# Two late pairs of experts trade their way of adding rows, the row additions come pair by pair in three buffers, and the token counts follow the first pair

## The chip, the core and the metric

The kernel runs on one core of one Trainium2 chip. The time is that of one execution on the device, in microseconds (us). A second clock value used below is the span: the time from the first to the last instruction that the profiler recorded.

## The reference, cut to what matters

Two transformer-like blocks work on a sequence of 512 tokens of width 1024, in f32. The first has attention, a recurrent branch and an MLP; the second has a Fourier and a state space branch and then a mixture of 64 experts. The change touches only the experts:

```
g_prob = softmax(ht @ wg + bg);  p_g, g_idx = top_k(g_prob, 1)          # one of 8 groups
e_logits = (ht @ we + be).reshape(t, 8, 8)                              # 8 experts in each
top_l, top_i = top_k(e_logits of the group, 2)                          # two experts a token
gate_w = p_g * softmax(top_l)
...
def expert_block(xb, e):
    a = silu(xb @ w_gate[e]) * (xb @ w_up[e])                           # 1024 -> 512
    return a @ w_down[e]                                                # 512 -> 1024
out = sum over the token's two experts of gate_w * expert's row
x = x + out;   return rms_norm(x)
```

There are 512 tokens with 2 experts each, so 1024 rows go through experts. Every expert has three matrices of 2 MB.

## The kernel before

**Pairs.** The 64 experts are worked on in 32 pairs, q = 0 to 31. An expert gets up to 64 rows (CAP), so that a pair fills 128 columns of TensorE. For a pair TensorE (in `pe_pair`) turns the gathered rows (`xt`), multiplies by the two gate matrices (`g`, 32 matmuls of 64 columns each, L1201), by the two up matrices (`u`, 32 more of L1201), turns the activated rows (`at`, L1212) and multiplies by the two down matrices (`d`, two halves nh = 0 and 1 of the 1024 columns, L1238; in the last pair L1226). VectorE scales `xt` (L2704, `dve_xt`), makes the gated product (L2709 and L2714), and copies half of the result to YE (`dve_ye`); ScalarE makes the tanh (L1679), copies `aT` (L1683) and the other half of YE (L1690).

**Weights.** SyncE's queue brings the matrices into a ring of ten slots of 2 MB (RING). Matrix n goes into its slot when TensorE has used matrix n - 10. The eleventh and twelfth come in pieces; the eleventh's first half goes to FIRST_HALF, a region that lies over constants which are no longer needed (from the constant `c01` on). That load (L3072) waits for the matmuls that count the tokens of each expert (`cnt`, L1133), since their operand `ones` lies in the region.

**Two ways to add a pair's rows.** For a pair in SPREAD, VectorE makes four one-hot matrices (`dve_hots`, L2647) and TensorE multiplies them with YE: 8 matmuls of 128x512, one for each half of each of four blocks of 128 tokens (`pe_spread`, L1172). VectorE adds each to the residual X (`dve_spread`, L2640). These 8 stand in the next pair's program: 4 ahead of its `g`, 2 between `u` and `at`, 2 between `at` and `d`; those of the last pair stand behind and between its own `d`. For a pair in STORED, GpSimd scatters YE to `y_d` in HBM by an indirect DMA (L2901, semaphore `y_st`). When all ten are written, GpSimd gathers the stored rows again (L2897): 8 indirect DMAs, one for each block of 128 tokens and each of the token's two experts; rows that belong to no stored pair are skipped. VectorE adds each gathered tile to X with its weight (`dve_comb`, L2631, 128x1024). GpSimd's queue also gathers each pair's tokens (L2897 from `hn_d`), except the first pair's, which come from one-hots.

**The end.** Before the change the 8 gathers start when the scatter of pair 30 has landed, into eight buffers YA; VectorE adds all 8 in the last pair (q = 31) ahead of adding the spread of pair 31. Then come the sums of squares, the scale and the stores of the output. The last pair's up matrices land as one load of 2 MB and two of 1 MB (semaphores `up0`, `up1`, `up2`, L3082 and L3085), its down matrices in six pieces (`last0` to `last2`, L3092).

```
STORED = [0, 2, 6, 10, 14, 18, 22, 26, 29, 30]
SPREAD = [q for q in range(PAIRS) if q not in STORED]
```

## Time and profile before

| | |
|---|---|
| time, median of 3 executions | 2291.91 us (2291.58 to 2294.2) |
| the profiled execution's own time | 2294.22 us |
| its span | 2292.3 us |
| TensorE busy, share of the span | 97% |
| VectorE, ScalarE, GpSimd busy | 43%, 15%, 13% |
| mean granted TensorE clock | 0.991 |
| HBM read and written | 558.63 MB and 24.67 MB |

The pairs of experts run from about 1345 us to 2276 us of the span. TensorE's busy share is that of a pipelined engine whose ends are modelled, so it tells only where it stands idle. In that stretch the granted clock and the share of the 16 DMA engines, by slices, say more.

### The profile page before, as it was taken

Reading aid. Unit: us, or ns where it says so; the run is one execution under the profiler, and the core shown is the slowest. Engines: PE = TensorE matmul, PEld = TensorE weight load, DVE = VectorE, ACT = ScalarE, POOL = GpSimd, SP = SyncE. Lnnn points to the kernel's source line nnn. Section 1 sums busy time; section 2 is a strip of 40 time slices with the busy share of each in tenths; the row PEclk is TensorE's granted clock in tenths of the full one; section 3 lists DMA queues with packets and bytes.
Section 4 is the critical chain, followed back from the end, with each engine's and each line's share of the span. In section 5 each row is a group of like instructions: output and inputs, shape, how many; then the busy total and the mean of one; then the engine's idle time right before and its main releaser. Section 6 shows DMA issues by size and latency. Waiting matters only on the chain.

```text
span 2292.3 us, 23432 instructions
## 1 busy us (share of the span) xinstructions
PE 2212.3 (97%) x9146; PEld 1140.7 (50%) x9146; DVE 974.5 (43%) x1888; ACT 349.0 (15%) x677; POOL 291.7 (13%) x254
## 2 busy tenths in 40 slices
PE   9999999999999999999999999999999999989996
PEld 6544444485888544477578553333333333333332
DVE  2246544541875587536544442222222222223124
ACT  2025324301222200021111210000000000000001
POOL 0002112221276100001053010000000000000001
PEclk9999999999999999999999999999999999999998
DMA  7211110230243444482432589999999999999996
GB/s 292 101 56 47 55 46 10 111 137 29 95 138 124 173 188 166 167 154 109 154 138 111 238 321 424 427 427 426 425 427 427 425 427 426 428 427 426 427 426 251
DMA packets 74991, 561.86 MB, mean 245 GB/s; under 512 B 20786, under 2 KB 25522, under 8 KB 42432
## 3 DMA queue, kind: packets, MB, share of 16 engines
q1 hardware_dynamic: 52688, 530.70, 57.8%
q10 hardware_dynamic: 15136, 22.75, 3.0%
q0 software_dynamic: 7056, 6.89, 0.9%
q8 instruction: 75, 1.23, 0.2%
q14 instruction: 36, 0.29, 0.0%
HBM read 558.63 MB, written 24.67 MB: 254 GB/s over the span
## 4 chain that ended last, share of the span: by engine, by line
PE 79%; DMA 13%; DVE 6%; issue 1%; ACT 1%; SPq 0%; POOL 0%; DVEq 0%; ACTq 0%; POOLq 0%
PE ps L1201 13%; DMA sb<-in_eu 11%; PE ps L527 9%; PE ps L855 8%; PE ps L1238 8%; PE ps L434 7%; PE ps L776 5%; PE ps L1172 5%; PE ps L1011 5%; PE ps L459 3%; PE ps L1039 2%; PE ps L737 2%; DVE sb L1717 2%; PE ps L715 2%; DMA sb<-in_ed 2%
## 5 line engine op out<-in xcount | busy, mean ns | idle before, releaser
L1201 PE MATMUL ps<-sb 128*64 128x512 f32 x2048 | 453.9, 599 | 22.6 <-DMA sb<-in_eu 17.4
L1201 PEld LDWEIGHTS ps<-sb 128*64 128x64 f32 x2048 | 156.6, 138 | 310.1 <-issue 310.1
L1717 DVE TENSOR_TENSOR sb<-sb 128x1024 f32<-128x1024 f32 (+9 forms) x420 | 226.9, 573 | 86.3 <-PE ps L855 38.3
L527 PE MATMUL ps<-sb 128*128 128x512 f32 x512 | 237.7, 602 | 0.0
L1238 PE MATMUL ps<-sb 128*64 128x512 f32 x992 | 224.5, 606 | 9.6 <-ACT sb L1683 5.5
L855 PE MATMUL ps<-sb 128*128 128x512 f32 x448 | 193.4, 592 | 1.4 <-DVE sb L2268 1.4
L434 PE MATMUL ps<-sb 128*128 128x512 f32 (+1 forms) x464 | 189.2, 567 | 0.9 <-issue 0.9
L776 PE MATMUL ps<-sb 128*128 128x256 f32 x784 | 175.5, 383 | 3.6 <-DVE sb L2188 3.6
L1172 PE MATMUL ps<-sb 128*128 128x512 f32 x352 | 164.6, 599 | 2.2 <-issue 2.2
L776 PEld LDWEIGHTS ps<-sb 128*128 128x128 f32 x784 | 148.4, 191 | 25.1 <-DVE sb L2188 4.0
L1238 PEld LDWEIGHTS ps<-sb 128*64 128x64 f32 x992 | 70.4, 139 | 154.3 <-issue 145.7
L527 PEld LDWEIGHTS ps<-sb 128*128 128x128 f32 x512 | 91.5, 191 | 101.3 <-issue 99.5
L855 PEld LDWEIGHTS ps<-sb 128*128 128x128 f32 x448 | 84.6, 190 | 106.7 <-issue 106.7
L2640 DVE TENSOR_TENSOR sb<-sb,ps 128x512 f32<-128x512 f32 x176 | 120.6, 688 | 38.8 <-PE ps L1172 38.5
L434 PEld LDWEIGHTS ps<-sb 128*128 128x128 f32 x464 | 87.5, 190 | 96.5 <-issue 92.7
L2709 DVE SCALAR_TENSOR_TENSOR sb<-sb,ps 128x512 f32<-128x512 f32 x32 | 22.1, 690 | 219.5 <-ACT sb L1679 219.4
L1011 PE MATMUL ps<-sb 128*128 128x256 f32 x504 | 109.2, 379 | 0.9 <-issue 0.9
L2714 DVE SCALAR_TENSOR_TENSOR sb<-sb,ps 128x512 f32<-128x512 f32 x32 | 22.1, 690 | 204.8 <-PE ps L1201 204.8
L2897 POOL DMA_INDIRECT sb<-hn_d,sb x31 | 31.1, 1005 | 582.1 <-PE ps L1183 548.0
L1011 PEld LDWEIGHTS ps<-sb 128*128 128x128 f32 x504 | 95.7, 190 | 14.6 <-issue 1.7
L1271 ACT ACTIVATE sb<-ps 128x512 f32<-128x512 f32 (+3 forms) x98 | 51.5, 535 | 321.4 <-PE ps L434 54.3
L1172 PEld LDWEIGHTS ps<-sb 128*128 128x128 f32 x352 | 61.8, 191 | 74.6 <-issue 74.6
(349 smaller groups left out, 2062.4 us busy)
## 6 DMA issues: line engine op xcount, KB each, us to landing
sb<-in_eu SPq DMA_DIRECT2D x63, 2048.0 KB, 33.9
sb<-in_eg SPq DMA_DIRECT2D x62, 2048.0 KB, 35.5
sb<-in_ed SPq DMA_DIRECT2D x60, 2048.0 KB, 33.7
sb<-in_m SPq DMA_DIRECT2D x16, 2048.0 KB, 7.3
sb<-in_m SPq DMA_DIRECT2D x16, 1024.0 KB, 4.9
sb<-in_mg SPq DMA_DIRECT2D x8, 1536.0 KB, 6.6
sb<-in_wo SPq DMA_DIRECT2D x4, 2048.0 KB, 7.9
sb<-in_winF SPq DMA_DIRECT2D x12, 512.0 KB, 3.5
```

What stands on the lines that cost most here:

```text
L434: ins = pe.matmul(out, lhsT, rhs, start=k == 0, stop=k == len(pieces) - 1)
L459: ins = pe.matmul(T.ap(*tile)[:, t], lhsT, rhs[:, t], start=k == 0, stop=k == 7)
L527: ins = pe.matmul(o, lhsT, rhs, start=k == 0, stop=k == 7)
L776: ins = pe.matmul(T.ap(*name)[:, 256 * (f % 2):256 * (f % 2) + 256], a[:, j], b[:, j], start=j == 0, stop=j == 3)
L855: ins = pe.matmul(T.ap("m2", turn, f), a[j], b[j], start=s_ == 0 and j == 0, stop=s_ == 7 and j == 1)
L1011: ins = pe.matmul(o[:, 256 * f:256 * f + 256], a[:, j], b[:, j], start=j == 0, stop=j == n - 1)
L1172: pe.matmul(o, OH[o_ % 2][:, i, :], YE[:, 512 * nh:512 * nh + 512], start=True, stop=True).then_inc(T.f("sp", q, i, nh), 1)
L1201: ins = pe.matmul(o[64 * e:64 * e + 64, :], x[:, k, 64 * e:64 * e + 64], weight(2 * mat + e, 512 * k), start=k == 0, stop=k == 7)
L1238: ins = pe.matmul(o[64 * e:64 * e + 64, :], aT[:, k, 64 * e:64 * e + 64], weight(4 + e, d), start=k == 0, stop=k == 3)
L1271: act.activation(dst, T.ap(*name) if src is None else src, ACT.Copy).then_inc(T.s(*name), 1)
L1717: return own(dve.tensor_tensor(o, a, b, op))
L2640: dve.tensor_tensor(xs, xs, T.ap("sp", q, i, nh), ALU.add).then_inc(S("xadd") if q == PAIRS - 1 else T.s("sp", q, i, nh), 1)
```

## The change

The list of stored pairs ends in 26, 27, 28, and no longer in 26, 29, 30. So pairs 27 and 28 are now scattered to HBM, and 29 and 30 are spread by one-hots; there are ten stored and 22 spread pairs as before. The 8 gathers of stored rows use three buffers in turn, and a gather waits until the addition that used its buffer is done. VectorE makes additions 0 to 2 in pair 29, 3 to 5 in pair 30, 6 and 7 in pair 31. The count matmuls move behind the first pair, and the VectorE operations that make the number of rounds of them (`count_rounds`) with them. The constant `ones` moves ahead of `c01`, out of the region under FIRST_HALF, and that load waits for TensorE's last read of the region (`rows_read`) instead of the counts.

```diff
-STORED = [0, 2, 6, 10, 14, 18, 22, 26, 29, 30]
+STORED = [0, 2, 6, 10, 14, 18, 22, 26, 27, 28]
...
-        YA = [view(done_ck, 0, 1024), view(done_ck, 1024, 1024), view(zone, xt0 + 1024, 1024), XG[0]]
-        YA += [view(EXTRA[0], 1024 * n, 1024) for n in range(4)]
+        YA = [view(done_ck, 0, 1024), view(done_ck, 1024, 1024), view(zone, xt0 + 1024, 1024)]
+        ROWS = {PAIRS - 3: range(3), PAIRS - 2: range(3, 6), PAIRS - 1: range(6, 8)}
...
+                    if i == 2 and k == 7:
+                        ins.then_inc(S("rows_read"), 1)
...
             first_rows(2, 1)
-            open_tile(pe, ("cnt",), 4)
-            for j in range(4):
-                ins = pe.matmul(T.ap("cnt")[:, 0:64], ck("ones"), ES[:, j, :], start=j == 0, stop=j == 3)
-            ins.then_inc(T.f("cnt"), 1)
...
                 if q == 0:
+                    o = open_tile(pe, ("cnt",), any_bank())
+                    for j in range(4):
+                        ins = pe.matmul(o[:, 0:64], ck("ones"), ES[:, j, :], start=j == 0, stop=j == 3)
+                    ins.then_inc(T.f("cnt"), 1)
                     o = open_tile(pe, ("wtab",), any_bank())
...
             def weights():
-                count_rounds()
...
                     copy(("wtab",), WTAB, T.ap("wtab")[:, 0:PAIRS])
+                    count_rounds()
...
             dve_xt(dve, T, q)
+            dve_spread(dve, q - 1, TILES[0:4])
             dve_gate(dve, T, q)
             dve_up(dve, T, q)
+            dve_spread(dve, q - 1, TILES[4:8])
             dve_hots(dve, q)
-            if len(SPREAD) > 1:
-                for i, nh in TILES:
-                    dve.wait_ge(*T.free("sp", SPREAD[-2], i, nh))
-            for n in range(8):
-                dve_comb(dve, n, S("comb"), YA[n], S(f"comb{n}"))
-            dve.wait_ge(S("comb"), 8)
+            dve_stored_rows(dve, q)
...
+                if q >= PAIRS - 3:
+                    dve.wait_ge(S("comb"), 8 if q == PAIRS - 1 else ROWS[q + 1].start)
...
+            if table is T and q in ROWS:
+                dve_stored_rows(dve, q)
             dve_ye(dve, table, q)
+
+        def dve_stored_rows(dve, q):
+            done = [p for p in SPREAD if p < q]
+            for i, nh in TILES:
+                dve.wait_ge(*T.free("sp", done[-1], i, nh))
+            for n in ROWS[q]:
+                dve_comb(dve, n, S("comb"), YA[n % 3], S(f"comb{n}"))
...
             for n in range(8):
-                if n == 4:
-                    pool.wait_ge(*T.full("u", PAIRS - 2))
-                gather(pool, YA[n], y_d, GY[:, n % 2, n // 2:n // 2 + 1], 1023, S(f"comb{n}"))
+                if n > 2:
+                    pool.wait_ge(S("comb"), n - 2)
+                gather(pool, YA[n % 3], y_d, GY[:, n % 2, n // 2:n // 2 + 1], 1023, S(f"comb{n}"))
...
-                    sp.wait_ge(*T.full("cnt"))
+                    sp.wait_ge(S("rows_read"), 1)
```

The first place is the end of TensorE's program. Before the change its rows for pairs 30 and 31 read as follows, where L1183 turns `xt`, L1201 is `g` with `u`, L1212 is `at`, L1238 and L1226 are `d`, and L1172 is a spread:

```order
L1183 MATMUL ps<-sb 128x128 x8
L1201 MATMUL ps<-sb 64x512 x32
L1212 MATMUL ps<-sb 128x128 x4
L1238 MATMUL ps<-sb 64x512 x16
L1183 MATMUL ps<-sb 128x128 x8
L1201 MATMUL ps<-sb 64x512 x32
L1212 MATMUL ps<-sb 128x128 x4
L1226 MATMUL ps<-sb 64x512 x8
L1172 MATMUL ps<-sb 128x512 x2
```

After the change (two lines further down in the file) the last pair's rows are these, and pair 30's begin in the same way:

```order
L1185 MATMUL ps<-sb 128x128 x8
L1174 MATMUL ps<-sb 128x512 x4
L1203 MATMUL ps<-sb 64x512 x32
L1174 MATMUL ps<-sb 128x512 x2
L1214 MATMUL ps<-sb 128x128 x4
L1174 MATMUL ps<-sb 128x512 x2
L1228 MATMUL ps<-sb 64x512 x8
L1174 MATMUL ps<-sb 128x512 x2
```

Eight spread matmuls have come into each of the pairs 30 and 31, and have gone out of pairs 28 and 29 (the rows of pair 29 now read as those of pair 30 before).

The second place is GpSimd's queue over the last pairs, where L2901 (now L2911) is a scatter and L2897 (now L2907) a gather. Before:

```order
L2897 DMA sb<-hn_d,sb 128x1024 x3
L2901 DMA y_d<-sb 1024x1024 x2
L2897 DMA sb<-y_d,sb 128x1024 x8
```

After the change:

```order
L2911 DMA y_d<-sb 1024x1024
L2907 DMA sb<-hn_d,sb 128x1024
L2911 DMA y_d<-sb 1024x1024
L2907 DMA sb<-hn_d,sb 128x1024
L2907 DMA sb<-y_d,sb 128x1024 x8
```

The last two scatters stand ahead of the last gather of a pair's tokens (pair 31's), and the eight gathers of stored rows follow right behind it, in pair 29's time.

The third place is VectorE's end, from the one-hots of the last pair on, where L2631 is an addition of stored rows. Before:

```order
L2647 TENSOR_SCALAR sb<-sb 128x128 x4
L2631 SCALAR_TENSOR_TENSOR sb<-sb 128x1024 x8
L2640 TENSOR_TENSOR sb<-sb,ps 128x512 x4
L2623 TENSOR_SCALAR sb<-ps,sb 128x512
L2640 TENSOR_TENSOR sb<-sb,ps 128x512 x4
```

After the change (L2648, L2630, L2641, L2622):

```order
L2648 TENSOR_SCALAR sb<-sb 128x128 x4
L2630 SCALAR_TENSOR_TENSOR sb<-sb 128x1024 x2
L2641 TENSOR_TENSOR sb<-sb,ps 128x512 x4
L2622 TENSOR_SCALAR sb<-ps,sb 128x512
L2641 TENSOR_TENSOR sb<-sb,ps 128x512 x4
```

Two of the eight additions are left there; three stand in pair 29 and three in pair 30, behind the one-hots of these pairs and ahead of the copy to YE.

## Rows read from the trace of the kernel before

**Rows 1.** The page: span, GB/s in 40 slices, the software queue, a load's landing.
```profile
span 2292.3 us, 23432 instructions
...
GB/s 292 101 56 47 55 46 10 111 137 29 95 138 124 173 188 166 167 154 109 154 138 111 238 321 424 427 427 426 425 427 427 425 427 426 428 427 426 427 426 251
...
q0 software_dynamic: 7056, 6.89, 0.9%
...
sb<-in_m SPq DMA_DIRECT2D x16, 2048.0 KB, 7.3
```
**Rows 2.** Timeline of TensorE in pair 29: start, time, line, operation.
```profile
2185.09 1.09 PE L1183 MATMUL ps<-sb 128*128 128x128 f32 x8
...
2189.55 13.95 PE L1201 MATMUL ps<-sb 128*64 128x512 f32 x64
...
2207.55 7.09 PE L1238 MATMUL ps<-sb 128*64 128x512 f32 x32
2214.56 1.09 PE L1183 MATMUL ps<-sb 128*128 128x128 f32 x8
```
**Rows 3.** The same in pairs 30 and 31; idle time before and its ending in brackets.
```profile
2224.86 7.09 PE L1201 MATMUL ps<-sb 128*64 128x512 f32 x32 [1.61 <-DMA sb<-in_eu]
...
2236.35 8.52 PE L1238 MATMUL ps<-sb 128*64 128x512 f32 x32 [2.73 <-DMA sb<-in_ed]
...
2246.40 7.09 PE L1201 MATMUL ps<-sb 128*64 128x512 f32 x32 [0.51 <-DVE sb L2704]
2254.03 7.09 PE L1201 MATMUL ps<-sb 128*64 128x512 f32 x32 [0.54 <-DMA sb<-in_eu]
...
2263.47 3.65 PE L1226 MATMUL ps<-sb 128*64 128x512 f32 x16 [0.69 <-ACT sb L1683]
...
2276.91 3.67 PE L1172 MATMUL ps<-sb 128*128 128x512 f32 x8 [1.34 <-issue]
```
**Rows 4.** DMA issues at 2215.1 and 2187.0 us: count, KB, us to landing.
```profile
sb<-in_eu SPq DMA_DIRECT2D x1, 1024.0 KB, 38.9
...
sb<-hn_d,sb POOLq DMA_INDIRECT x1, 11.0
```
**Rows 5.** Windows: busy time of each engine, granted clock, DMA share, GB/s.
```profile
1340.00:1350.00 10.00, 10.00 (x67) 6.39 (x68) 8.48 (x38) 0.32 (x2) 1.02 (x2) 1.00 0.98 393
...
2180.00:2235.00 55.00, 50.55 (x225) 19.05 (x220) 12.23 (x18) 3.68 (x6) 2.00 (x2) 1.00 1.01 427
2235.00:2240.00 5.00, 3.65 (x12) 1.31 (x14) 0.00 (x0) 0.00 (x0) 0.00 (x0) 0.66 1.00 426
...
2260.00:2265.00 5.00, 3.37 (x18) 1.36 (x16) 3.66 (x7) 0.60 (x1) 4.05 (x3) 1.00 1.01 374
2265.00:2270.00 5.00, 4.16 (x16) 1.26 (x14) 4.58 (x5) 2.18 (x3) 1.10 (x1) 1.00 0.47 147
```
**Rows 6.** Timeline of VectorE and GpSimd from 2254 us on.
```profile
2254.86 1.03 POOL L2897 DMA_INDIRECT sb<-y_d,sb  x1 [7.50 <-DMA y_d<-sb]
...
2262.62 11.02 DVE L2631 SCALAR_TENSOR_TENSOR sb<-sb 128x1024 f32<-128x1024 f32 x8
...
2276.06 0.75 DVE L2623 TENSOR_SCALAR sb<-ps,sb 128x512 f32<-128x512 f32 x1
```
**Rows 7.** Timeline of all engines ahead of the first pair.
```profile
1340.86 1.00 PE L1133 MATMUL ps<-sb 128*128 128x64 f32 x8
...
1341.83 0.29 DVE L2553 TENSOR_TENSOR sb<-sb 128x128 f32<-128x128 f32 x1
...
1342.26 2.02 PE L1095 MATMUL ps<-sb 128*128 128x128 f32 x16
...
1345.24 0.22 DVE L2575 TENSOR_REDUCE sb<-ps 128x1 f32<-128x64 f32 x1
...
1345.87 0.15 DVE L2579 TENSOR_SCALAR sb<-sb 128x1 int32<-128x1 int32 x1
```
**Rows 8.** DMA issues at 1378.4 us, behind the gate matmuls of pair 1.
```profile
sb<-in_ed SPq DMA_DIRECT2D x2, 2048.0 KB, 11.3
```

More of the change, by code:

```diff
@@ L41 @@
 CK_COLS = {}
-CK_N = _cols(CK_COLS, [("ident", 128), ("iota", 128), ("tok", 8), ("gf", 8), ("gx", 8), ("kept", 32), ("c01", 124), ("tri", 128), ("ones", 128),
+CK_N = _cols(CK_COLS, [("ident", 128), ("iota", 128), ("tok", 8), ("gf", 8), ("gx", 8), ("kept", 32), ("ones", 128), ("c01", 124), ("tri", 128),
                        ("neg", 128), ("cneg", 124), ("cs", 256), ("pad", 40)])
```

## The prediction

> **What bounds the kernel now.** I read the page first, for the traffic in 40 slices; then the timeline of TensorE over the last three pairs, for what it waits for; then the landings of the loads, and the timelines of VectorE and GpSimd at the end. From the 25th slice on the DMA engines move 425 to 428 GB/s in every slice but the last [rows 1], and in the windows their share is 1.01 [rows 5]: they are full. TensorE's waits in pairs 30 and 31 are ended by the weights: 1.61 us ahead of `u` and 2.73 ahead of `d` in pair 30, 0.54 ahead of `u` in pair 31 [rows 3]. A load of the last pair lands 38.9 us after its issue [rows 4], so the queue holds over 30 us of work and TensorE can be late by some us without leaving it empty. So the end of the kernel hangs on when the last pair's first up pieces land, and on what TensorE still has to do from there. VectorE and GpSimd matter only where they hold up this chain.
>
> From `u` of pair 31 at 2254.03 us it runs to `d` at 2263.47 [rows 3], 9.44 us later, and from there 28.8 us to the end of the span at 2292.3. I keep this last part as it is, but for one item below, and ask by how much the start of the last `d` moves.
>
> **The change part by part.**
>
> *Gathers of stored rows, moved ahead of the last weights.* Before, the first of 8 is issued at 2254.86 [rows 6], when the up matrices that `u` needs have landed (2215.1 + 38.9 = 2254.0 [rows 4]). They take bandwidth only from the last down matrices, and no wait of the last `d` is put down to these [rows 3]. After, the last scatter (pair 28) lands two pairs earlier, and gathers 0 to 2 run in pair 29, 3 to 5 behind the first additions, 6 and 7 behind those of pair 30. A gather lands 11.0 us after its issue while the loads take over 30 [rows 4]: it doesn't queue behind them but takes its share at once. All 8 thus come ahead of the last up pieces, 6 of them ahead of pair 30's down matrices. The two scatters that move were ahead of these before too and cost the same.
>
> Their size: GpSimd's queue moves 6.89 MB [rows 1]. The gathers of tokens of pairs 1 to 31 are 31/32 of 1024 rows of 4 KB, 4.06 MB; the other 2.83 MB are scatters and gathers of the same stored rows, 1.41 MB each. At the stream's 427 GB/s that is 3.3 us. At this queue's own use of the engines, 0.9% of 2292.3 us for 6.89 MB or 3.0 us a MB [rows 1], it is 4.2 us. No row isolates them in a full stream, so I take the middle, 3.7. The same queue's mixed window at the end, 374 GB/s at a share of 1.01 [rows 5], says that the upper half is no less likely.
>
> The Trainium skill, "DMA: Bandwidth & Descriptors", section "Anatomy of one DMA", fits the moving part of a DMA by bytes at 436 GB/s, which would make 3.2 us of the 1.41 MB and an end 0.5 us earlier than by my 3.7; the 374 GB/s above, with much small traffic in it, disagree.
>
> *Spreads in pairs 30 and 31.* The lists of instructions show 8 more matmuls in each, and 8 fewer in pairs 28 and 29, which wait for weights anyway or gain time that is lost again at the next landing. The price is read from pair 29, which has them: from the start of L1183 to `g` 4.46 us (2185.09 to 2189.55), from `g` to `d` 18.00 (2189.55 to 2207.55), from `d` to the next L1183 7.01 [rows 2]. From the start of `u` to `d` it is 18.00 less half of L1201's 13.95, 11.03 us, against 9.44 without spreads: 1.6 more.
>
> *The sum, by two chains.* By the weights: `u` of pair 31 at 2254.03 + 3.7 = 2257.7, and `d` 11.03 later, at 2268.8. By TensorE: `d` of pair 30 at 2236.35 + 3.7 x 6/8 = 2239.1, next L1183 + 7.01, `g` + 4.46, `d` + 18.00, together 29.47: 2268.6. Both agree, so neither covers the other. The last `d` comes at 2268.8 instead of 2263.47: **+5.3**. In pair 30 TensorE itself is not what holds `d`: pair 29 without spreads ends earlier than before.
>
> *Eight additions of VectorE.* Before they are one block of 11.02 us up to 2273.64, 1.38 each; behind it come four spreads, and the copy of the second half of YE starts at 2276.06 [rows 6], though its matmuls had ended at 2276.91 - 1.34 = 2275.57 [rows 3]. With two additions left that copy follows at once, about 0.1 us after the matmuls: **-0.4**. In pairs 29 and 30 three additions, 4.1 us, stand ahead of the copy to YE. The spread that reads it comes 7.01 + 1.09 = 8.1 us after `d` starts [rows 2], which leaves 4 us for the one-hots and the copy: nothing, while the gathers have landed.
>
> *The first load of the ring's third round.* It is issued when the counts have ended, some 0.9 us later than it could be (1.00 us of L1133 [rows 7]). But at that time the DMA share is 0.98 [rows 5], and the next pieces wait for TensorE's first pair. That pair doesn't start earlier: the matmuls at 1342.26 need the product of VectorE that ends at 1342.12 [rows 7]. I take 0; the other end is -0.9, the whole stream moved.
>
> *The counts behind pair 0.* TensorE's 1.00 us and VectorE's, from 1345.24 to 1346.02, 0.8 us [rows 7], now both stand ahead of pair 1's `g`: up to 1.8 us. The load that waits for these gate matmuls goes at 1378.4. Two loads into an empty queue would land 7.3 us and 7.3 + 4.9 after their issue (2 MB at 427 GB/s are 4.9), on the median 9.75; they took 11.3 [rows 1, 8], so 1.55 us were queued ahead. So 0.2 us of the stream may be lost: **+0.2**, between 0 and 1.8. The lateness of TensorE itself goes away in its later waits for weights.
>
> Together 5.3 - 0.4 + 0.2 = **+5.1 us**: the profiled execution would go from a span of 2292.3 to 2297.4 and from its own 2294.2 to 2299.3. That execution was the slowest of the three and 2.3 above their median; on the median 2291.91 it makes **2297.0**. With the gathers at 3.3 us the sum is +4.7, at 4.2 it is +5.6.
>
> **The rivals.**
>
> *A, on the other side: the gathers take nothing from the weights* (they use gaps within packets that a share of 1.01 doesn't show). Then TensorE's chain decides: 2236.35 + 29.47 = 2265.8, +2.35, less 0.4, makes 2293.9, which is no change that can be told. For it speaks that the engines' share is a sum of packet times and can count waiting; against it that GB/s doesn't rise when this queue has work [rows 5]. It decides from a cost of the gathers below 3.2 us: under that the total is under 4.6. Chance 0.20.
>
> *B, the clock.* Between 2235 and 2240 the granted clock averages 0.66 [rows 5], after idle stretches of 1.61 and 2.73 us; `d` of pair 30 ran 8.52 us, not 7.09 [rows 3]. The 7.01 above is at full clock. If half clock comes again there, or in pair 31, it is on the path now and costs 1.4: 2298.4. TensorE has less idle time in pair 30 than before, some 2 us ahead of `u`, which speaks against it. Chance 0.17.
>
> *C, additions that wait for their gathers.* If gathers 0 to 2 land too late for pair 29, VectorE holds up the copy to YE, with it the spread of pair 29 and `g` of pair 30. Beyond some 2 us this reaches `u`: 2299. Against it: 11.0 us a gather from the middle of pair 29's time still leaves some. Chance 0.06.
>
> *D, the stream moves with its first load* by the full 0.9 and nothing else changes: 5.1 - 0.2 - 0.9 = +4.0, 2295.9. Against it the share of 0.98. Together with other gains that I don't see, some even beyond, chance 0.07.
>
> **How the numbers follow.** A measurement of this kernel tells about 0.2%, 4.6 us, from no change; the three runs lie 2.6 us apart. The forecast has 0.50; as its sum runs from +4.7 to +5.6, and a run can come out half a us to one us otherwise, I give 0.37 of it to slower and 0.13 to within 0.2%. A is within (0.20), B and C are slower (0.23), of D and unseen gains 0.03 is within and 0.04 faster. So faster 0.04, same 0.36, slower 0.60. The range is 2293.4 to 2299.6: from a little below A, 2293.9, to B's 2298.4 and C's 2299.
>
> **What would show it.** Gathers of `y_d` issued around 2195 to 2245 us, and none behind the last up pieces. Ahead of `u` of pair 31 a wait that the weights end, or none, at about 2257.8; the last `d` at about 2269, 11 us later. The DMA traffic's end near 2268 as before. VectorE's copy of the last half right behind its matmuls. I would be wrong if `u` of pair 31 still began near 2254 to 2256 (the gathers cost little), if half clock stood in the last pairs, or if the landings from pair 3 on had moved by more than 0.5 us either way (the start of the stream).

## The result: slower by 14 us, and the profile after

The changed kernel took 2306.83 us in the median of five executions, the kernel before 2291.91: a ratio of 1.0061, with a 95% interval of 1.0048 to 1.0073, so slower by 11 to 17 us. One of the five took 5037.78 us; it is left out of the ratio, and the median of the other four (2305.22 to 2309.09) is 2306.44. I had forecast 2297.0 and a range up to 2299.6. The direction was right, the size was not: 5.1 us forecast, 14 measured. In a second measurement the same kernel took 2304.12 us against 2293.04, a ratio of 1.0040 [1.0026, 1.0054], or 9 us (the last experiment below). Both intervals lie above the 1.0022 of the forecast.

The profiled execution has its own time 2305.22 and a span of 2303.2 us, 10.9 more than the 2292.3 of before [rows 1]. It was the fastest of the changed kernel's, and before's was the slowest of its own, so the spans show less than the medians. The page of after, three of its lines:

```profile
span 2303.2 us, 23440 instructions
...
GB/s 291 100 55 47 55 46 10 113 151 10 110 131 132 164 178 182 182 153 114 115 137 115 237 357 426 426 426 426 426 426 426 427 426 426 427 427 427 427 423 186
...
q0 software_dynamic: 7056, 7.28, 0.9%
```

The stream of weights is as full as before [rows 1]. What is new stands in the timeline of TensorE (start, time, line, operation, idle time before it and what ended it); L1240 and L1228 are `d`, L1185 `xt`, L1174 a spread, L1203 `g` and `u`:

```profile
2205.84 9.97 PE L1240 MATMUL ps<-sb 128*64 128x512 f32 x32 [2.42 <-DMA sb<-in_ed]
2215.74 1.09 PE L1185 MATMUL ps<-sb 128*128 128x128 f32 x8
2222.22 5.22 PE L1174 MATMUL ps<-sb 128*128 128x512 f32 x8 [5.38 <-issue]
2227.37 13.95 PE L1203 MATMUL ps<-sb 128*64 128x512 f32 x64
...
2245.36 7.09 PE L1240 MATMUL ps<-sb 128*64 128x512 f32 x32
...
2274.84 3.66 PE L1228 MATMUL ps<-sb 128*64 128x512 f32 x16
```

The last `d` starts at 2274.84, where I had 2268.8, and before 2263.47 [rows 3]. Before the spread of pair 29's rows TensorE stands still for 5.38 us, put down to "issue": the profile has no releaser for it. VectorE's timeline (L2648 one-hots, L2630 an addition of stored rows, L2730 the copy to YE that this spread reads, L2622 the last such copy) says who it was:

```profile
2202.47 0.87 DVE L2648 TENSOR_SCALAR sb<-sb 128x128 f32<-128x128 f32 x4
2209.89 1.28 DVE L2630 SCALAR_TENSOR_TENSOR sb<-sb 128x1024 f32<-128x1024 f32 x1 [6.56 <-DMA sb<-y_d,sb]
2214.89 1.28 DVE L2630 SCALAR_TENSOR_TENSOR sb<-sb 128x1024 f32<-128x1024 f32 x1 [3.71 <-DMA sb<-y_d,sb]
2220.17 1.28 DVE L2630 SCALAR_TENSOR_TENSOR sb<-sb 128x1024 f32<-128x1024 f32 x1 [3.99 <-DMA sb<-y_d,sb]
2221.37 0.74 DVE L2730 TENSOR_SCALAR sb<-ps,sb 128x512 f32<-128x512 f32 x1
...
2286.98 0.75 DVE L2622 TENSOR_SCALAR sb<-ps,sb 128x512 f32<-128x512 f32 x1 [1.19 <-PE ps L1228]
```

Three additions, and each waits for its gather; the copy runs at 2221.37, and TensorE's spread starts 0.85 us later. The views of single DMA issues, at 2198.4, 2199.7 and 2201.0 us, and of the up loads issued at 2216.2 (count, KB, us to landing):

```profile
sb<-y_d,sb POOLq DMA_INDIRECT x1, 11.4
...
sb<-y_d,sb POOLq DMA_INDIRECT x1, 15.2
...
sb<-y_d,sb POOLq DMA_INDIRECT x1, 19.2
...
sb<-in_eu SPq DMA_DIRECT2D x1, 1024.0 KB, 40.7
```

The three are issued 1.3 us apart and land 5.1 and 5.3 us apart: 2209.8, 2214.9, 2220.1. The first of the two 1 MB up pieces, which the last `u` needs, lands at 2216.22 + 40.7 = 2256.9, 2.9 us later than before [rows 4], where I had 3.7. It is no longer waited for: TensorE runs from 2227.37 to the end of `u` without a wait for weights.

The windows show one thing more (time, busy PE, PEld, DVE, ACT, POOL, then granted clock, DMA share, GB/s):

```profile
2200.00:2235.00 35.00, 26.25 (x98) 9.64 (x95) 9.93 (x15) 1.78 (x3) 4.64 (x5) 0.85 1.01 423
2235.00:2240.00 5.00, 5.00 (x26) 1.71 (x24) 0.69 (x1) 0.10 (x1) 0.00 (x0) 1.00 1.02 430
```

Before, the clock of this stretch was full, and the drop came in 2235 to 2240 [rows 5]. Now it is down in pair 29: `d` there runs 9.97 us, not 7.09, and the spread behind the hold 5.22 us. The same part of a spread (the four matmuls ahead of `g`, each two in the profile, so x8) at the full 2.4 GHz takes 3.60 (the kernel with two blocks, below), so the hold cost 5.38 us of standing and 1.62 of lower clock, 7.0 us together.

### The profile page after: what moved, and what is told of

It reads as the page before. It is cut to its first block, busy times and chain, and to the rows that moved or that the text cites. A ratio compares the mean times of both kernels' runs of the same rounds, so it can differ in the third digit from the quotient of the medians.

```text
span 2303.2 us, 23440 instructions
## 1 busy us (share of the span) xinstructions
PE 2220.5 (96%) x9146; PEld 1141.8 (50%) x9146; DVE 974.5 (42%) x1888; ACT 349.3 (15%) x677; POOL 291.1 (13%) x254
## 3 DMA queue, kind: packets, MB, share of 16 engines
q0 software_dynamic: 7056, 7.28, 0.9%
## 4 chain that ended last, share of the span: by engine, by line
PE 80%; DMA 11%; DVE 6%; issue 1%; ACT 1%; SPq 0%; POOL 0%; DVEq 0%; ACTq 0%; POOLq 0%
PE ps L1203 14%; PE ps L527 9%; PE ps L855 8%; PE ps L1240 8%; PE ps L434 7%; DMA sb<-in_eu 5%; PE ps L1174 5%; PE ps L776 5%; PE ps L1011 5%; DMA sb<-in_ed 4%; PE ps L459 3%; PE ps L1039 2%; PE ps L737 2%; DVE sb L1719 2%; PE ps L715 2%; DMA sb<-in_eg 2%
## 5 line engine op out<-in xcount | busy, mean ns | idle before, releaser
L1203 PE MATMUL ps<-sb 128*64 128x512 f32 x2048 | 454.5, 601 | 19.3 <-DMA sb<-in_eu 12.8
L1203 PEld LDWEIGHTS ps<-sb 128*64 128x64 f32 x2048 | 155.4, 138 | 308.6 <-issue 308.4
L1240 PE MATMUL ps<-sb 128*64 128x512 f32 x992 | 230.9, 620 | 10.0 <-ACT sb L1685 6.2
L1174 PE MATMUL ps<-sb 128*128 128x512 f32 x352 | 166.2, 604 | 7.1 <-issue 7.1
L1240 PEld LDWEIGHTS ps<-sb 128*64 128x64 f32 x992 | 71.7, 142 | 159.2 <-issue 149.7
L2641 DVE TENSOR_TENSOR sb<-sb,ps 128x512 f32<-128x512 f32 x176 | 120.9, 687 | 44.6 <-PE ps L1174 44.5
L1174 PEld LDWEIGHTS ps<-sb 128*128 128x128 f32 x352 | 62.5, 193 | 80.6 <-issue 80.6
L2907 POOL DMA_INDIRECT sb<-hn_d,sb x31 | 31.2, 1007 | 524.0 <-PE ps L1185 490.6
```

The source lines that it names most:

```text
L1174: pe.matmul(o, OH[o_ % 2][:, i, :], YE[:, 512 * nh:512 * nh + 512], start=True, stop=True).then_inc(T.f("sp", q, i, nh), 1)
L1203: ins = pe.matmul(o[64 * e:64 * e + 64, :], x[:, k, 64 * e:64 * e + 64], weight(2 * mat + e, 512 * k), start=k == 0, stop=k == 7)
L1240: ins = pe.matmul(o[64 * e:64 * e + 64, :], aT[:, k, 64 * e:64 * e + 64], weight(4 + e, d), start=k == 0, stop=k == 3)
L2641: dve.tensor_tensor(xs, xs, T.ap("sp", q, i, nh), ALU.add).then_inc(S("xadd") if q == PAIRS - 1 else T.s("sp", q, i, nh), 1)
```

## The experiments

Executions of one kernel differ by some 2 to 8 us, and whole streams lie some us earlier or later in one execution than in another. So beside the ratio I use a length inside the trace: from the start of `d` of pair 29 to the start of the last `d`, as the differences of the two starts in TensorE's timeline. It comes from one execution of each kernel, whose own time stands beside the median. The change's two traces agree in it to 0.14 us; before and counts only, which took the same time, differ by 0.9, so differences under some 1 us are not read.

| kernel | median us | profiled us | ratio to before, 95% | `d`(29) to last `d` |
|---|---|---|---|---|
| before | 2291.91 | 2294.22 | 1 | 55.92 |
| the change | 2306.83 | 2305.22 | 1.0061 [1.0048, 1.0073] | 69.00 |
| the change again | 2304.12 | 2308.52 | 1.0040 [1.0026, 1.0054] | 69.14 |
| counts only | 2294.17 | 2294.34 | 1.0000 [0.9991, 1.0009] | 56.81 |
| spread of pair 29 only | 2293.10 | 2293.91 | 0.9998 [0.9990, 1.0007] | 57.33 |
| no gathers, pairs 30 and 31 spread | 2297.02 | 2297.02 | 1.0015 [1.0006, 1.0024] | 60.46 |
| no gathers, pairs 29 to 31 spread | 2297.54 | 2298.07 | 1.0021 [1.0012, 1.0030] | 60.07 |
| two blocks of additions | 2300.08 | 2299.85 | 1.0029 [1.0019, 1.0040] | 62.20 |
| one addition in pair 29 | 2300.80 | 2294.49 | 1.0031 [1.0020, 1.0042] | 62.17 |
| copy first | 2301.74 | 2296.76 | 1.0035 [1.0023, 1.0047] | 63.85 |
| three additions in pair 29 | 2304.93 | 2302.12 | 1.0052 [1.0040, 1.0064] | 65.53 |
| all additions last | 2304.08 | 2304.08 | 1.0045 [1.0031, 1.0059] | 62.48 |
| stored one pair earlier | 2303.88 | 2303.55 | 1.0046 [1.0030, 1.0061] | 61.02 |
| 8 KB packets | 2301.70 | 2302.36 | 1.0035 [1.0024, 1.0047] | 63.53 |
| 4 KB packets | 2304.59 | 2299.03 | 1.0046 [1.0033, 1.0060] | 63.22 |
| before with 4 KB packets | 2296.70 | 2297.28 | 1.0010 [1.0001, 1.0019] | 59.42 |

The medians of before measured beside them were 2293.0 to 2293.5, and 2291.9 beside the change.

### The parts of the change

**Counts only.** The kernel before with the counts behind pair 0, and the stored pairs, buffers and additions as they were:

```diff
 # the kernel before, and of the change only:
-            open_tile(pe, ("cnt",), 4)
...
-                    sp.wait_ge(*T.full("cnt"))
+                    sp.wait_ge(S("rows_read"), 1)
```

> The kernel before with only the counts moved behind pair 0, the constant moved and the first load of the ring's third round waiting for the last read of the region. Forecast: 0 to +0.2 us. If the whole stream moves with that load, -0.9 us; if the later gate matmuls of pair 1 starve the queue, up to +1.8 us. Landings up to pair 3 tell which.

The ratio was 1.0000, so the start of the change costs nothing that can be told; the interval is 2 us to either side and holds all of my 0 to 1.8. The traces say where such a cost would go: `d` of pair 1 starts 1.9 us later than before (1389.55 against 1387.64) and `d` of pair 4 still does, but the last pair's first 1 MB up piece lands at 2253.9 here and at 2254.0 before.

**No gathers.** The changed kernel without its eight gathers and the additions that use them, so its output lacks the rows of the ten stored pairs:

```diff
-            for n in ROWS[q]:
-                dve_comb(dve, n, S("comb"), YA[n % 3], S(f"comb{n}"))
...
-                gather(pool, YA[n % 3], y_d, GY[:, n % 2, n // 2:n // 2 + 1], 1023, S(f"comb{n}"))
```

> The changed kernel without the 8 gathers of stored rows and without their additions, so that the stored pairs' rows are missing in the output; the scatters stay. Theory H with the forecast's sum: no hold and no bytes taken from the weights. TensorE's chain decides: the last down matmuls near 2266, up matrices of the last pair land 3.5 to 4 us earlier than in the changed kernel (2256.9), so near 2253, span 2293.5 to 2295. Rival R: still 2300 or more, since the spreads are there.

1.0021, 4.8 us over before: without any gather the moved spreads alone cost this much, more than theory H had (its span of 2293.5 to 2295 was 2296.1), and below the 2300 of rival R. It may be a little more, since this kernel also lacks the eight additions that made before's last copy 0.5 us late [rows 3, 6]. In the changed kernel the gathers and what waits for them add the rest.

What the gathers themselves take from the weights shows against two kernels further down (two blocks, all additions last), which have them and no hold in pair 29. The first 1 MB up piece of the last pair took 40.0 us to land without gathers (issued at 2215.17), 43.4 with two blocks (2214.76) and 43.7 with all additions last (2214.46). So the gathers cost 3.4 to 3.7 us of the stream, as forecast. The software queue moves 7.28 MB with them and 5.70 without, so they are 1.58 MB (at 427 GB/s 3.7 us), 0.2 MB each.

**Spread of pair 29 only, and of pair 30 only.** First the kernel before with pair 28 stored in the place of 29; then the kernel without gathers with pair 29 stored in the place of 27, so that 30 and 31 are spread:

```diff
-STORED = [0, 2, 6, 10, 14, 18, 22, 26, 29, 30]
+STORED = [0, 2, 6, 10, 14, 18, 22, 26, 28, 30]
 # the second, from the kernel without gathers
-STORED = [0, 2, 6, 10, 14, 18, 22, 26, 27, 28]
+STORED = [0, 2, 6, 10, 14, 18, 22, 26, 28, 29]
```

> The kernel before with pair 28 stored in the place of pair 29 (stored 26, 28, 30), and nothing else. Theory L (only work behind the last weights' landing counts): pair 29's spread lies in pair 30, where TensorE waited 1.61, 0.94 and 2.73 us, and pair 31 stays as it was: ratio to the kernel before 0.9990 to 1.0010, 0 to 1 us. Rival H (each spread moved late costs its share of the 4.8 us of the kernel without gathers): ratio 1.0008 to 1.0015, 2 to 3 us.

> The changed kernel without its eight gathers and additions (its output lacks the stored rows), with pairs 26, 28 and 29 stored, so that of the last pairs only 30 and 31 are spread. Theory L: the spread of pair 30's rows in pair 31 adds some 3 to 4.5 us behind the landing of the last weights of `up`, whatever is done with pair 29: ratio to the kernel before 1.0013 to 1.0022, as the kernel without gathers (1.0021). Rival H: half of it, 1.0008 to 1.0013.

0.9998 [0.9990, 1.0007] and 1.0015: pair 29's spread costs nothing that can be told, and pair 30's 3.4 us [1.4, 5.5], most of the 4.8 of both; the intervals of the two kernels without gathers overlap. TensorE's rows from `d` of pair 30 on in the kernel with pair 29 alone:

```profile
2238.05 7.09 PE L1238 MATMUL ps<-sb 128*64 128x512 f32 x32
2245.07 1.09 PE L1183 MATMUL ps<-sb 128*128 128x128 f32 x8
2246.67 13.95 PE L1201 MATMUL ps<-sb 128*64 128x512 f32 x64 [0.51 <-DVE sb L2704]
...
2262.97 3.65 PE L1226 MATMUL ps<-sb 128*64 128x512 f32 x16 [0.69 <-issue]
```

and in the one with pair 30:

```profile
2237.23 7.09 PE L1240 MATMUL ps<-sb 128*64 128x512 f32 x32 [0.69 <-ACT sb L1685]
2244.24 1.09 PE L1185 MATMUL ps<-sb 128*128 128x128 f32 x8
2245.18 3.60 PE L1174 MATMUL ps<-sb 128*128 128x512 f32 x8
2248.71 13.95 PE L1203 MATMUL ps<-sb 128*64 128x512 f32 x64
...
2266.70 3.65 PE L1228 MATMUL ps<-sb 128*64 128x512 f32 x16
```

From `d` to the last `d` it is 24.92 us in one and 29.47 in the other. In pair 30 the spread fills time in which TensorE waited for weights (1.61 and 2.73 us before [rows 3]); in pair 31 only 0.54 of such waiting was left. In the kernel with pair 29 alone `d` of pair 29 ran at a lower clock, 10.02 us and not 7.09, and that too was lost in these waits.

### The hold in pair 29

**All additions last.** The changed kernel, with eight buffers and all eight additions in the last pair, as before:

```diff
+        YA = [view(done_ck, 0, 1024), view(done_ck, 1024, 1024), view(zone, xt0 + 1024, 1024), XG[0]]
+        YA += [view(EXTRA[0], 1024 * n, 1024) for n in range(4)]
-        ROWS = {PAIRS - 3: range(3), PAIRS - 2: range(3, 6), PAIRS - 1: range(6, 8)}
+        ROWS = {PAIRS - 1: range(8)}
...
-                if n > 2:
-                    pool.wait_ge(S("comb"), n - 2)
+                if n == 3:
+                    pool.wait_ge(*T.full("xt", PAIRS - 2, 1))
+                if n == 4:
+                    pool.wait_ge(*T.full("u", PAIRS - 2))
```

> The changed kernel, but all 8 additions of stored rows stand in the last pair again, with eight buffers; gathers 0 to 2 still go in pair 29, the fourth when pair 30's xt is made, the rest behind pair 30's up matrices. Theory H (VectorE is held by additions that wait for their gathers: in the changed kernel's trace they end at 2221.5 and TensorE idles 5.4 us ahead of pair 30's spread): that idle time goes, gate of pair 30 begins near 2218 to 2219 instead of 2227.4, the last down matmuls near 2269 instead of 2274.8, and the span is 2297 to 2298.5. Rival R (the eight more spread matmuls in each of pairs 30 and 31 and the gathers' bytes cost the 11 us themselves): the span stays at 2302 to 2304.

The hold was gone, as theory H had it: the last `d` at 2269.44, 62.48 us after that of pair 29. But the span was 2302.1, in rival R's range and not in H's. VectorE's rows at the end:

```profile
2270.94 11.02 DVE L2631 SCALAR_TENSOR_TENSOR sb<-sb 128x1024 f32<-128x1024 f32 x8
2282.09 2.48 DVE L2642 TENSOR_TENSOR sb<-sb,ps 128x512 f32<-128x512 f32 x4
2284.49 0.75 DVE L2623 TENSOR_SCALAR sb<-ps,sb 128x512 f32<-128x512 f32 x1
```

The copy comes at 2284.49, when its matmuls had ended at 2281.54; before it was late by 0.5 us only [rows 3, 6]. For with a spread of pair 30 in the last pair the additions start 1.50 us after the last `d` (2269.44 to 2270.94), while before they started 0.85 us ahead of it (2262.62 against 2263.47 [rows 3, 6]). TensorE's idle time ahead of the last spreads was 3.80 us, and they ran partly at half clock, 5.10 us for 3.67. From the last `d` to the end of the span it is 32.7 us here and 28.4 in the change. So by these two traces moving additions out of the last pair was worth 4.3 us to the changed kernel, not my 0.4. This trade I had not seen.

**Stored one pair earlier.** Pairs 25, 26 and 27 stored, the first three gathers in pair 28:

```diff
+STORED = [0, 2, 6, 10, 14, 18, 22, 25, 26, 27]
...
+                if q == PAIRS - 4:
...
+                    for n in range(3):
+                        gather(pool, YA[n], y_d, GY[:, n % 2, n // 2:n // 2 + 1], 1023, S(f"comb{n}"))
```

> The changed kernel with pairs 25, 26, 27 stored as the last (not 26, 27, 28) and the first three gathers issued in pair 28, ahead of the gather of pair 31's tokens; three buffers and additions 0 to 2, 3 to 5, 6 and 7 in pairs 29 to 31 as in the changed kernel. Theory H: the first three gathers land before pair 29's additions, no hold there, span 2297 to 2299. It may hold elsewhere if gather 3 to 5 land late. Rival R: spreads in pairs 29, 30, 31 are even one pair more, span 2302 or more. A second rival (VectorE's own 4 us of additions ahead of the copy to YE is the cost, not the landings): 2301 to 2304 here too.

No hold either, and 61.02 us from `d` to `d`, though here too VectorE makes three additions ahead of pair 29's copy: their gathers had landed. But the span was 2301.5, not the 2297 to 2299 of theory H, and the ratio 1.0046: pair 29's `d` starts at 2212.14 here and not at 2205.84. Pair 29 now has pair 28's spread in it, and the stream of this execution lay some 4 us later than in the change. As a test of the hold by the time it is inconclusive.

**Copy first.** The additions of pairs 29 and 30 behind the copy to YE:

```diff
+            dve_ye(dve, table, q)
             if table is T and q in ROWS:
                 dve_stored_rows(dve, q)
-            dve_ye(dve, table, q)
```

> The changed kernel with VectorE's additions of pairs 29 and 30 behind its copy of the results, not ahead of it. Theory V (the additions that wait for gathers hold VectorE, and VectorE holds TensorE): the copy comes at 2212 instead of 2221.4, but the token copy of pair 30 then stands behind the additions that wait to 2221, so g(30) starts at 2221 to 2223 instead of 2227.4, the last `d` 2269 to 2272 instead of 2274.8, span 2298 to 2301. Rival T (the lost time lies in TensorE's own work at half clock or in the weights, not in what VectorE waits for): 2302.5 to 2304, as the change.

The median was 2301.74, a ratio of 1.0035. As expected the wait goes to the next thing behind the additions, the tokens of pair 30, and is smaller there:

```profile
2213.55 3.60 PE L1174 MATMUL ps<-sb 128*128 128x512 f32 x8
2218.99 13.96 PE L1203 MATMUL ps<-sb 128*64 128x512 f32 x64 [1.83 <-DVE sb L2714]
```

The spread runs at once and at full clock. The profiled execution was the fastest of six, 5 us below the median: its span, 2294.8, lies below what I had expected, and its whole stream was some 3 us early; from `d` to `d` it is 63.85.

**Two blocks.** Eight buffers, rows 0 to 3 at the end of pair 30, rows 4 to 7 ahead of the first spread additions of pair 31:

```diff
+        ROWS = {PAIRS - 2: range(4), PAIRS - 1: range(4, 8)}
...
             dve_xt(dve, T, q)
+            dve_stored_rows(dve, q)
             dve_spread(dve, q - 1, TILES[0:4])
```

> The changed kernel with eight buffers again (all eight gathers one after another, 3 to 7 behind TensorE's pair 30) and the additions in two blocks where VectorE has nothing due: rows 0 to 3 at the end of pair 30, rows 4 to 7 ahead of the first half of the spread of pair 30's rows in pair 31. The pairs stored and spread are those of the change. Theory V: no hold in pair 29, and no late last copy as with all eight additions in the last pair: last `d` 2268 to 2270, the last copy right behind it, span 2296.5 to 2299, 2 to 4 us below that with all additions last (2302.1). What is then left over the kernel before (4 to 6 us) is the price of spreading pairs 29 and 30 on TensorE and VectorE. Rival T: 2301 or more. If the gathers of rows 4 to 7 land later than 2262, the gate of pair 31 waits for them and the span is 2300 to 2303.

2300.08 us, 1.0029, span 2297.8, as theory V has it. TensorE's rows; nothing is held, and weights are what `u` waits for in both pairs:

```profile
2215.22 3.60 PE L1175 MATMUL ps<-sb 128*128 128x512 f32 x8
...
2228.12 7.09 PE L1204 MATMUL ps<-sb 128*64 128x512 f32 x32 [2.28 <-DMA sb<-in_eu]
...
2258.34 7.09 PE L1204 MATMUL ps<-sb 128*64 128x512 f32 x32 [0.52 <-DMA sb<-in_eu]
...
2269.47 3.65 PE L1229 MATMUL ps<-sb 128*64 128x512 f32 x16
```

**One and three additions in pair 29.** Two blocks again, with one of the first four, or three, moved into pair 29:

```diff
-        ROWS = {PAIRS - 2: range(4), PAIRS - 1: range(4, 8)}
+        ROWS = {PAIRS - 3: range(1), PAIRS - 2: range(1, 4), PAIRS - 1: range(4, 8)}   # or 3
```

> The kernel with two blocks of additions, with one of the first block's four moved into pair 29, ahead of its copy of the results. Theory V (what an addition costs is the landing of its gather against the copy that stands behind it): the first gather lands at 2207.8 to 2209.8, the addition ends 1.4 us later, ahead of the end of pair 29's first half of results (about 2211), so nothing is held: median within 1.5 us of two blocks (2300.1), last `d` 2268 to 2270. Rival M (any addition in pair 29 costs, by its time on VectorE or by the wait for the spreads before it): 2 to 3 us more.

> The same with three additions in pair 29, as the change has them, but with eight buffers. Theory V: they wait to 2219.5 to 2221.5 for the third gather, TensorE waits 4.5 to 5.5 us ahead of its spread, and since it had 2.3 us of waits for weights behind that place in the kernel with two blocks, the last `d` moves by 2.5 to 4 us: median 2302.5 to 2304.5 against 2300.1. Rival B3 (it is the three buffers, which hold gathers 3 to 7 back, that cost): median as with two blocks, 2299 to 2301.5.

With one: 2300.80 us, 62.17 from `d` to `d`, no different from two blocks. (The profiled execution was the fastest of seven, with its stream early; its `d` of pair 29 ran 9.77 us at a lower clock, which here cost nothing, since TensorE waited 0.30 us for weights behind it where it waited 2.28 and 0.52 with two blocks.) The gather has landed and the copy waits for TensorE (VectorE's rows):

```profile
2204.42 1.28 DVE L2631 SCALAR_TENSOR_TENSOR sb<-sb 128x1024 f32<-128x1024 f32 x1 [4.96 <-DMA sb<-y_d,sb]
2208.28 0.75 DVE L2733 TENSOR_SCALAR sb<-ps,sb 128x512 f32<-128x512 f32 x1 [2.58 <-PE ps L1241]
```

With three: 2304.93 us, 4.1 more on the same chip, and 65.53 from `d` to `d`. The intervals of the two ratios just touch (1.0040 to 1.0042); their difference, 0.0021, is some 0.0005 to 0.0037, an estimate from the two intervals. TensorE's rows:

```profile
2219.18 5.12 PE L1175 MATMUL ps<-sb 128*128 128x512 f32 x8 [4.90 <-issue]
2224.23 13.95 PE L1204 MATMUL ps<-sb 128*64 128x512 f32 x64
```

So it is not additions in pair 29 as such, nor the three buffers, but the landing of the second and third gather. What else sets the change apart from this kernel (three buffers, the places of the other additions), 65.53 against 69.00, was not tested by itself.

### Why the gathers land five us apart

**4 KB and 8 KB packets.** The changed kernel, with the twelve loads that are in flight at the time issued as four or as two column pieces, so that a row of weights goes in packets of 4 or 8 KB, not 16; and the same on the kernel before:

```diff
+    if name == "ex" and 176 <= g < 188:
+        return 4      # 2 for packets of 8 KB
...
-                sp.dma_start(slot(*name)[:, 0:n], src).then_inc(s, 16)
+                k = pieces(*name) if name[0] == "ex" else 1
+                for c in range(0, n, n // k):
+                    sp.dma_start(slot(*name)[:, c:c + n // k], src[:, c:c + n // k]).then_inc(s, 16)
```

> The changed kernel, with the twelve weight loads that are in flight while the stored rows are gathered (matrices 176 to 187, pairs 29 to 31) issued as four column pieces each, so that a row goes in 4 KB packets, not 16 KB. Theory Q: a gather of 128 rows is 8 packets in each DMA engine, and each stands behind one packet of the weights (16 KB of 427/16 GB/s are 0.6 us, 8 of them 4.9 us, the 5 us at which the gathers land one after another); then with 4 KB packets they should land 1.3 to 2.5 us apart, the third at 2211 to 2215 rather than 2220.1, the additions of pair 29 end at 2212 to 2216, and TensorE's 5.4 us of waiting ahead of its spread goes to under 2: span 2297 to 2299. Rival K: a gather costs what it costs by its rows or by GpSimd's queue, whatever the packets beside it: still 5 us apart, span 2302 to 2304. Rival S: more DMAs in the weights' queue slow the weights themselves: the last weights of `up` land later than 2258 and the span is over 2304 even where the gathers come sooner.

> Control: the kernel before with the same twelve loads in four pieces. It has no addition in the middle that waits for a gather, so by theory Q the time stays (2291 to 2293.5 in the span), and its scatter and gathers at 2215 to 2240 land sooner. Rival S (more DMAs slow the weights): over 2294. Rival K: same span, and the landings of the indirect DMAs as before (8.8 us the scatters, 11.0 the token gather).

> The changed kernel with the same twelve weight loads in two column pieces each, so that a row goes in 8 KB packets. It is the middle step between the change (16 KB, gathers landing 5.0 to 5.3 us apart) and the kernel with 4 KB packets (8.3, 8.5 and 8.9 us from issue to landing). Theory Q (each of a gather's 8 packets in a DMA engine stands behind one packet of the weights): the second and third gather land 2.3 to 3.0 us behind the one before, the third 11 to 14 us after its issue, and TensorE waits 0 to 2 us ahead of pair 29's spread. Rival N (the number of queued DMAs decides, not the packet's size): the distance lies near that of 4 KB packets, under 2 us, or stays at 5. For the median theory Q gives 2299 to 2303, since pieces themselves cost something (the kernel before with four pieces: 1.0010).

The first three gathers, each issue by itself, with 8 KB packets (issued at 2194.01, 2195.30 and 2196.60):

```profile
sb<-y_d,sb POOLq DMA_INDIRECT x1, 9.3
...
sb<-y_d,sb POOLq DMA_INDIRECT x1, 10.8
...
sb<-y_d,sb POOLq DMA_INDIRECT x1, 12.3
```

and with 4 KB packets (issued at 2191.28, 2192.57 and 2193.87):

```profile
sb<-y_d,sb POOLq DMA_INDIRECT x1, 8.3
...
sb<-y_d,sb POOLq DMA_INDIRECT x1, 8.5
...
sb<-y_d,sb POOLq DMA_INDIRECT x1, 8.9
```

They land 5.1 and 5.3 us apart with 16 KB, 2.8 and 2.8 with 8 KB, 1.5 and 1.7 with 4 KB, where GpSimd's own issues are 1.3 apart, so that the last step is near the least that could show. The distance goes with the size of the pieces, as theory Q had it; rival K, a fixed cost of a gather, and rival N as it was put (under 2 us, or still 5) are out. A DMA engine moves 427/16 = 26.7 GB/s [rows 5]; eight rows of 16 KB through it take 4.9 us, of 8 KB 2.5, of 4 KB 1.2. The 128 rows of a gather, and of a load, are eight for each of 16 engines if they are spread evenly. So the distance is about the time of eight rows of weights, and it is not the gather's own bytes: 0.2 MB are 0.5 us of the stream. (The eight gathers are 7056 - 5904 = 1152 packets of the software queue, 144 each, but only rows that belong to a stored pair are moved.) One thing changes along with the size: the weights' queue gets shorter. Loads issued at 2189 to 2200 us took 40.1 us to land in the change, 30.6 with 8 KB and 14.7 with 4 KB. From 16 to 8 KB the queue is down by a quarter and the distance by nearly half, which fits the rows better; from 8 to 4 KB both are down by half, and nothing here parts them. Whether row alternates with row, as my expectation put it, or one whole gather with one whole load or piece, these runs can't tell: both readings give the same distances. The Trainium skill, "DMA: Bandwidth & Descriptors", section "Queues, rings and completion order", says that an engine takes turns between its queues packet by packet, a packet there being several descriptors; the distances agree with turns of eight rows, and no run here shows where a packet ends.

The distance is no constant of the kernel either: with two blocks of additions the gathers 4 to 7, issued 1.3 us apart from 2235.98 on, when the last pair's smaller pieces were in the queue, landed 5.7, 4.0 and 3.0 us apart.

With either size the hold is gone: TensorE's spread follows `xt` directly, and from `d` to `d` it is 63.5 and 63.2 us. The times are less kind. The pieces themselves cost the kernel before 2.3 us (1.0010, and a span of 2295.2, so rival S holds as far as that). From 2190 to 2240 us the traffic was 408 GB/s with them and 427 before; over 50 us that is 2.2 us. With 8 KB the changed kernel took 2301.70, within my 2299 to 2303, and 2.4 us less than the change on the same chip, but the two intervals overlap almost wholly. With 4 KB it took 2304.59; its profiled execution, 2299.03, was its fastest. That median is above the 2299 to 2301 that my span meant. Two blocks' 6.6 us with 2.3 for the pieces would be 1.0039, within its 1.0033 to 1.0060; whether the other executions had a hold no trace shows.

**The change again.** The changed kernel unaltered, on the chip of the 8 KB packets (so its edit is empty).

> The changed kernel unaltered, so that its ratio stands beside the others' on one chip. From its own five runs: ratio 1.0048 to 1.0073, median 2305 to 2309, and in its trace the third gather of the stored rows landing 17 to 20 us after its issue with TensorE waiting 4 to 6 us ahead of pair 29's spread. If the ratio came out under 1.0040, the hold would be worth less than the kernels without it say.

1.0040, below the 1.0048 to 1.0073 that I had expected and on the edge that I had named. The profile, of the slowest of its five executions, repeats the first and shows a longer stretch of half clock:

```profile
2208.98 8.78 PE L1240 MATMUL ps<-sb 128*64 128x512 f32 x32 [2.38 <-DMA sb<-in_ed]
...
2224.00 6.72 PE L1174 MATMUL ps<-sb 128*128 128x512 f32 x8 [5.21 <-issue]
```

The hold is there in every trace of a kernel that issues the first gathers in pair 29, makes three additions there ahead of the copy and has 16 KB packets (4.90, 5.21, 5.38 us), and in no other. Its worth in time is less sharp: 14.0 and 9.2 us over before in the two measurements of the change and 11.9 with three additions and two blocks. The kernels that shorten or avoid it are at 6.6 (two blocks), 7.1 (one addition), 8.0 (copy first), 8.0 (8 KB), 10.3 (all additions last), 10.5 (stored earlier) and 10.5 (4 KB). The first of the three at 10 us loses 4.3 at its late last copy, the third some 2.3 by its pieces, and for the second nothing of the kind is known; by the ratios alone these three are not told apart from the change's second measurement. On one chip, three additions against one, the hold is worth 4.1 us.

## Why the prediction was wrong, point by point

- **The step that failed.** "In pairs 29 and 30 three additions, 4.1 us, stand ahead of the copy to YE. ... nothing, while the gathers have landed." The gathers had not landed. Behind it stood "A gather lands 11.0 us after its issue": true of one gather alone (11.4 measured for the first), but I used it for three in a row. They took 11.4, 15.2 and 19.2 us, so the third addition came at 2220.17 and the copy at 2221.37, 15.5 us after the start of `d`, where with two blocks it came 3.7 us after it. My sum had nothing for this wait; it measured 5.38 us of standing and 1.62 of lower clock.
- **The row that I had and passed over.** Rows 4 shows a token gather in a queue by itself. At 2124.1 and 2125.5 us the same trace has a scatter and a gather one right after the other, and they took 11.3 and 15.3 us:

```profile
y_d<-sb POOLq DMA_INDIRECT x1, 11.3
...
sb<-hn_d,sb POOLq DMA_INDIRECT x1, 15.3
```

  The second lands 5.3 us after the first. To ask how two indirect DMAs behave together, before pricing three, would have given rival C its true size.
- **Rival C** named the mechanism and the place ("beyond some 2 us this reaches `u`: 2299"), with a chance of 0.06. The hold was 5.38 us and came with 1.62 of lower clock. By TensorE's chain the last `d` came at 2274.84 for my 2268.8: 6.0 us, of which 2299 had room for 2.
- **Rival B**, half clock: it did come, in pair 29 and not in 30, behind waits of 2.42 and 5.38 us. In `d` of pair 29 it costs nothing by itself: it stood there too with pair 29's spread alone (10.02 us, ratio 0.9998) and with one addition (9.77 us, as fast as two blocks). The account against two blocks closes with it: 2.88 us more for `d` of pair 29, 5.38 of hold and 1.62 behind it are 9.9, less the 2.28 and 0.52 us that TensorE with two blocks waits for weights and the change doesn't, 7.1; measured from `d` to `d` are 69.00 - 62.20 = 6.8.
- **The weights' chain (gather bytes)**: the up piece landed 2.9 us later, forecast 3.7, but such landings lie up to 7 us apart between traces of kernels with the same gathers (2252.8 to 2260.1), so the time from issue to landing is the better measure: 40.0 us without gathers, 43.4 and 43.7 with them. The 3.7 was right, and rival A, that the gathers take nothing, is out by this. (I had 1.41 MB, it was 1.58; and in the change the last two gathers land at 2257.1 and 2260.1, behind that up piece and not ahead of it.) Two blocks over no gathers, which have the same spreads, is 1.8 us by the ratios, whose intervals overlap, and 2.1 from `d` to `d`.
- **The spreads by TensorE's chain.** I had 2236.35 + 29.47, which is 2.35 us, as what they cost alone. The kernel without gathers shows 4.8 [2.8, 6.9]. In its trace `d` of pair 30 came at 2238.27, since pair 30 too had a spread and a wait of 0.90 for weights; from `d` of pair 29 a chain without waits needs twice 29.47, 58.9 us, 3.0 more than before's 55.92. The 2.35 was too small for that reason; the rest up to 4.8 lies within the interval.
- **The sum without the hold.** Two blocks is the change as I had forecast it, with no hold and no late last copy: +6.6 us [4.4, 9.2] against +5.1, the wait for weights ahead of `u` of pair 31 ending at 2258.34 (forecast 2257.7) and the last `d` at 2269.47 (2268.8). So the sum was good for a kernel that the change was not.
- **-0.4 for the last copy** was right in the changed kernel: VectorE's idle time ahead of it is ended by TensorE, and the span ends 28.4 us after the last `d`, against 28.8 before. What I missed is that with eight additions left there it would have been 32.7.
- **The start** (first load, counts): 1.0000 [0.9991, 1.0009], which fits the forecast of +0.2 and could not have told it from 0 or 1.8.

No version here beats the kernel before. The best with pair 30 spread and the output complete is two blocks, 6.6 us behind it; the parts that cost nothing (counts, pair 29's spread) gain nothing either.

## What to carry to other kernels

A landing time read from one DMA is no price for three in a row: look for two of its kind issued together, and take the distance between landings as the price of each further one; beside a full stream of large loads that distance was here about eight rows of the stream, and it fell with the size of the pieces. An operation that may wait for a DMA belongs behind whatever another engine needs from the same queue, or at a place that comes later than the worst landing. And work that was free in a pair that waits for weights (pair 29's spread) cost 3.4 us in the last pair, where hardly any such wait was left: try it in each place by itself.

## What the runs showed of the hardware that I had not expected

- Indirect DMAs of 128 rows, of which 0.2 MB move, issued 1.3 us apart beside a stream of 427 GB/s, land 5.1 to 5.3 us apart when the stream's rows are 16 KB, 2.8 at 8 KB and 1.5 to 1.7 at 4 KB. All traffic together hardly changed by it (423 GB/s from 2200 to 2235).
- Each time that TensorE stood still for some 5 us, the spread behind (x8 in the profile) took 5.12, 5.22 and 6.72 us where 3.60 are usual: the wait costs 1.5 to 3.1 us more than it lasts. In the change the granted clock was 0.72 from 2222 to 2228, so part of it ran at 1.2 GHz, and 1.00 from 2228 to 2240.
- The same twelve loads in four pieces each cost the kernel before 2.3 us [0.2, 4.4]: the traffic was 408 GB/s from 2190 to 2240 and not 427, and the first 1 MB up piece of the last pair landed 2.9 us later in the profile (2256.9 against 2254.0).
